# A modulated norm at the head of a two-block transformer kernel: who multiplies the rows of the modulation matrix, and in which order its panels are loaded

## What is computed

```
cond = silu(c)                                    # 1024 values
mod = cond @ w_ada + b_ada                        # w_ada is 1024 x 6144; six parts of 1024
sh1, sc1, gt1, sh2, sc2, gt2 = split(mod, 6)
h = rmsnorm(x, g_mix) * (1 + sc1) + sh1
proj = h @ w_in                                   # its first product: columns C_CQ.., "lat"
```

## Time and profile before

| | |
|---|---|
| median of 3 runs | 796.71 us (796.2 to 798.56) |
| the profiled execution's own time | 800.01 us |
| its span, first to last instruction | 798.0 us |
| PE busy | 95% of the span |
| mean granted clock of PE | 0.981 of full speed |

### The profile page before, as it was taken

One profiled execution on the slowest core, in us unless ns is written; L12 is line 12 of the kernel. 1 busy time (PEld: TensorE's weight loads), 2 busy tenths in 40 slices (PEclk: granted clock), 3 DMA queues, 4 the chain that ended last, 5 costly groups with the idle time before them and its releaser, 6 DMA issues.

```text
span 798.0 us, 14672 instructions
## 1 busy us (share of the span) xinstructions
PE 754.5 (95%) x5310; PEld 691.0 (87%) x5310; DVE 555.9 (70%) x1071; ACT 439.5 (55%) x831; POOL 63.8 (8%) x94
## 2 busy tenths in 40 slices
PE   3699999999999999999999999979899999999997
PEld 3699897899999899999999888867798999999997
DVE  3976449898897866666566755469776877776773
ACT  5327466665645555545545647377665555555452
POOL 8001011000445000000000030000000000000000
PEclk9799999999999999999999999999899999999999
DMA  9977797888796566657657294422153666566531
GB/s 297 346 208 241 188 216 230 266 271 274 253 290 193 146 198 192 194 167 198 195 165 179 58 241 133 139 80 80 54 148 117 211 193 193 166 198 192 167 100 54
DMA packets 186933, 148.24 MB, mean 186 GB/s; under 512 B 13662, under 2 KB 171296, under 8 KB 186872
## 3 DMA queue, kind: packets, MB, share of 16 engines
q1 hardware_dynamic: 183008, 143.61, 61.1%
q10 hardware_dynamic: 2232, 3.03, 2.0%
q0 software_dynamic: 1648, 1.00, 0.5%
HBM read 146.29 MB, written 1.36 MB: 185 GB/s over the span
## 4 chain that ended last, share of the span: by engine, by line
PE 83%; DVE 8%; ACT 5%; issue 2%; DMA 1%; POOL 0%; ACTq 0%; DVEq 0%; POOLq 0%
PE ps L2139 19%; PE ps L1765 15%; PE ps L1766 14%; PE ps L1767 14%; PE ps L2141 10%; DVE w_lo L1135 2%; ACT w_hi L696 1%; DMA arena<-in_x 1%; PE ps L2009 1%; PE ps L2216 1%; PE ps L1831 1%; PE ps L2031 1%; DVE sq L1276 1%; PE ps L1813 1%; PE ps L1996 1%
## 5 line engine op out<-in xcount | busy, mean ns | idle before, releaser
L1135 DVE TENSOR_TENSOR w_lo<-raw,w_hi 128x1024 fp32r<-128x1024 f32 (+3 forms) x223 | 271.1, 1237 | 84.9 <-ACT w_hi L696 83.7
L2139 PE MATMUL ps<-h,w_hi 128*128 128x512 f32 x672 | 239.4, 396 | 0.0
L696 ACT ACTIVATE w_hi<-raw 128x1024 fp32r<-128x1024 f32 (+3 forms) x223 | 226.4, 1038 | 23.3 <-PE ps L1767 13.3
L2141 PE MATMUL ps<-h,w_lo 128*128 128x256 f32 x672 | 189.5, 282 | 0.0
L2139 PEld LDWEIGHTS ps<-h,w_hi 128*128 128x128 f32 x672 | 126.3, 188 | 28.6
L1765 PE MATMUL ps<-h,w_hi 128*128 128x256 f32 (+1 forms) x472 | 137.9, 292 | 5.1 <-ACT bias L1034 1.2
L1766 PE MATMUL ps<-h,w_hi 128*128 128x256 f32 (+1 forms) x472 | 134.1, 284 | 0.0
L1767 PE MATMUL ps<-h,w_lo 128*128 128x256 f32 (+1 forms) x472 | 133.6, 283 | 0.0
L2141 PEld LDWEIGHTS ps<-h,w_lo 128*128 128x128 f32 x672 | 126.2, 188 | 0.0
L1765 PE MATMUL ps<-g_hi,w_hi 128*128 128x256 f32 x352 | 98.7, 280 | 2.6 <-DVE g_lo L1467 2.6
L1765 PEld LDWEIGHTS ps<-h,w_hi 128*128 128x128 f32 (+1 forms) x472 | 90.3, 191 | 10.1 <-issue 7.4
(11 more groups left out here) (353 smaller groups left out, 1120.4 us busy)
## 6 DMA issues: line engine op xcount, KB each, us to landing
raw<-in_w_in SPq DMA_DIRECT2D x53, 512.0 KB, 5.4
raw<-in_w_down SPq DMA_DIRECT2D x44, 512.0 KB, 4.3
raw<-in_w_gate_up SPq DMA_DIRECT2D x44, 512.0 KB, 4.1
raw<-in_w_ada SPq DMA_DIRECT2D x32, 512.0 KB, 4.7
raw<-in_w_gate SPq DMA_DIRECT2D x22, 512.0 KB, 4.0
raw<-in_w_up SPq DMA_DIRECT2D x22, 512.0 KB, 5.1
raw<-in_w_ada SPq DMA_DIRECT2D x32, 256.0 KB, 5.9
raw<-in_w_o SPq DMA_DIRECT2D x8, 512.0 KB, 4.8
```

The costliest lines, as they stand in the source:

```text
L696: A(w_hi[:, m % HL, 0:w], raw[:, n % RAW, 0:w], ACT.Copy).then_inc(hi_done, 1)
L1135: V.tensor_tensor(w_lo[:, m % HL, 0:w], raw[:, n % RAW, 0:w], w_hi[:, m % HL, 0:w].bitcast(f32), sub).then_inc(lo_done, 1)
L2139: T.matmul(bank[:, :], hi, h2[:, k, :, :].rearrange("p a b -> p (a b)"), start=(k == 0), stop=False, skip_group_check=True)
L2141: ins = T.matmul(bank[:, 0:SEQ], lo, h_hi[:, k, :], start=False, stop=(k == KC - 1), skip_group_check=True)
```

## The change

The prologue has three pieces, `PIECES = ((0, 3), (3, 6), (6, 8))`, and a different engine multiplies the rows of each:

- **Piece 0**: eight panels of one row chunk each (768 columns, 393 KB). PE takes rows 0, 2, 4, 6 itself (`first_mod`: the 128x128 blocks of the row as weights, `cond` spread over 128 columns as the moving side), DVE takes rows 1, 3, 5, 7 (`mod_part`); `first_sums` adds DVE's part on PE.
- **Piece 1**: eight such panels, all by DVE, then `second_sums`.
- **Piece 2**: four panels of two rows (512 columns), all by PE (`last_mod`).

The loads come in this order: eight rows of piece 0, `lat0`; three rows of piece 1, `lat1`; three rows, `lat2`; two rows; four panels of piece 2, `lat3`; `lat4` to `lat7`.

PE's order is rows 0 and 2, transposes of `x`, row 4, `rows_t`, `factor`, row 6, `first_sums`, `lat0` to `lat2`, two panels of piece 2, `second_sums`, two panels of piece 2, `lat3`, `lat4`, the bias products, `lat5`, `lat6`, `lat7`. `keep_awake` is not called any more in the prologue.

`c` gets a load and a transpose of its own, ahead of the others; `x` is issued before `b_ada` and `g_mix`; ACT loads its tables for Silu and Sqrt by a dummy call each; the copies of `x` out of PSUM move from ACT to DVE. `scaled` and `low0` become `normal` (x times the inverse norm, made without waiting for the gain) and `h_piece` (sum with gain and shift, then the low part), and ACT makes `h_hi` from the normal and the gain by itself. Elsewhere only semaphores are merged or dropped.

The core of the diff:

```diff
-PIECES = ((0, 2), (2, 4), (4, 6), (6, 7), (7, 8))
+PIECES = ((0, 3), (3, 6), (6, 8))
+MOD_N = (8, 8, 4)
+LAT_PANELS = ((8,), (3, 6), (4,))
...
+        by_pe = q == 2 or (q == 0 and n % 2 == 0)
...
+    done = 0
+    for q in range(len(PIECES)):
+        for n in range(MOD_N[q]):
+            ada_piece(q, n)
+            if n + 1 in LAT_PANELS[q]:
+                lat_panels(done, done + 1)
+                done += 1
+    lat_panels(done, KC)
```

In ACT's program:

```diff
+            split.ahead(0 - AHEAD)
+            for q, (a, b) in enumerate(PIECES):
+                act.wait_ge(s("gain_ready"), q + 1)
+                for c in range(a, b):
+                    line(A(h_hi[:, c, :], sq[:, c, :], ACT.Identity, scale=gs[:, 0, c:c + 1], bias=mod[:, 0, c:c + 1]),
+                         "h_hi")
+                if q < 2:
+                    split.ahead(2 + q - AHEAD)
+            split.ahead(5 - AHEAD)
             act.wait_ge(s("frow_mm"), 2)
...
+            split.ahead(7 - AHEAD)
```

In DVE's program:

```diff
+            for m in mods_of[0][1:4:2]:
+                mod_part(m)
+            for b in range(4):
+                dve.wait_ge(s("x_t"), b + 1)
+                line(V.tensor_copy(xT[:, 2 * b:2 * b + 2, :].rearrange("p a b -> p (a b)"), ps[b][:, :]), "x_copied")
+            inverse(0)
+            for m in mods_of[0][5:8:2]:
+                mod_part(m)
...
+            for c in range(*PIECES[0]):
+                normal(c)
+            split.ahead(0 - AHEAD)
+            dve.wait_ge(s("va_ready"), 1)
+            gain_shift(0)
+            h_piece(0)
+            split.ahead(1 - AHEAD)
+            for m in mods_of[1][0:3]:
+                mod_part(m)
+            split.ahead(2 - AHEAD)
+            for m in mods_of[1][3:8]:
+                mod_part(m)
+            for c in range(*PIECES[1]):
+                normal(c)
+            gain_shift(1)
+            h_piece(1)
+            split.ahead(3 - AHEAD)
+            for c in range(*PIECES[2]):
+                normal(c)
+            gain_shift(2)
+            h_piece(2)
+            split.ahead(7 - AHEAD)
```

In PE's program:

```diff
+            def first_mod(k):
+
+                n = direct_of[k]
+                pe.wait_ge(raw_in[n % RAW], raw_count[n])
+                for x in range(3):
+                    for out_, at_ in ((GAIN0, x * P), (SHIFT0, (3 + x) * P)):
+                        ins = T.matmul(out_[:, x * P:(x + 1) * P], raw[:, n % RAW, at_:at_ + P],
+                                       cond[:, k:k + 1].to_broadcast([P, P]), start=(k == 0 and x == 0), stop=False,
+                                       skip_group_check=True)
+                ins.then_inc(first_used, 1)
+
+            def last_mod(m):
+
+                n, (_, k0, kn, w) = direct_of[m], mod_panels[m]
+                pe.wait_ge(raw_in[n % RAW], raw_count[n])
+                pe.wait_ge(s("gain_ready"), 1)
+                for j in range(kn):
+                    for x in range(4):
+                        ins = T.matmul(ps[4][:, x * P:(x + 1) * P], raw[:, n % RAW, j * w + x * P:j * w + (x + 1) * P],
...
-            for q in range(1, len(PIECES)):
-                mod_sums(q)
-                for k in range(*PIECES[q - 1]):
-                    lat_panel(k)
-                if q <= 2:
-                    keep_awake(ps[6], 2)
```

More of the change, by code:

```diff
@@ L59 @@
 TOKW = GROUP + 2 * HD + FOX_HEADS + 3 * NSA_HEADS
-VA = {"b_ada": 0, "g_mix": 48, "c": 56}
-VA_ROWS = 64
+VA = {"b_ada": 0, "g_mix": 48}
+VA_ROWS = 56
 VB = {"g_ffn": 0, "g_final": 8, "norm_mix_2": 16, "norm_ffn_2": 24, "out_norm_2": 32, "g_q_lora": 40,
@@ L311, in build @@
         x_tm = take(TT, D, start=0)
+        h_sum = arena[:, 0:KC * SEQ].rearrange("p (a b) -> p a b", b=SEQ)
         va_rows = take(P, rows=VA_ROWS)
+        c_rows = take(P, rows=KC)
         vb_rows = take(P, rows=VB_ROWS)
@@ L745, in highs @@
                     high(k, c, shift)
-            split.ahead(AHEAD_OF[1][-1] - AHEAD)
-            act.wait_ge(s("frow_mm"), 2)
[L749 to L757, removed]
+            split.ahead(0 - AHEAD)
[7 more added lines that the diff above has]
+            split.ahead(5 - AHEAD)
+            act.wait_ge(s("frow_mm"), 2)
+            line(A(bias[0:A_HEADS, 0, :], ps[5][0:A_HEADS, 0:FW], ACT.Copy))
+            line(A(bias[0:NSA_HEADS, 1, :], ps[6][0:NSA_HEADS, 0:FW], ACT.Copy), "frow_copied")
+            act.wait_ge(s("rows_t"), 3)
+            line(A(vb[:, :], ps[7][:, 0:VB_ROWS], ACT.Copy), "vb_ready")
+            split.ahead(7 - AHEAD)
             act.wait_ge(s("arg_ready"), 1)
@@ L1178, in mod_part @@
             def mod_part(m):
-                n, (q, k0, kn, w) = direct_of[m], mod_panels[m]
+                n, (q, k, _, w) = direct_of[m], mod_panels[m]
                 dve.wait_ge(raw_in[n % RAW], raw_count[n])
[L1182 to L1192, removed]
+                src, dst = raw[:, n % RAW, 0:w], mod_acc[:, q, :]
@@ new lines, in normal, with h_piece @@
+            def normal(c):
+                line(V.tensor_tensor(sq[:, c, :], xT[:, c, :], NRM, mult))
+            def h_piece(q):
+                a, b = PIECES[q]
+                line.settle()
+                for c in range(a, b):
+                    line(V.tensor_scalar(h_sum[:, c, :], sq[:, c, :], gs[:, 0, c:c + 1], mod[:, 0, c:c + 1], mult, add), "h_ready")
+                for c in range(a, b):
+                    dve.wait_ge(s("h_ready"), c + 1)
+                    dve.wait_ge(s("h_hi"), c + 1)
+                    line(V.tensor_tensor(h_lo[:, c, :], h_sum[:, c, :], h_hi[:, c, :].bitcast(f32), sub), "h_lo")
@@ new lines, in first_sums, with second_sums @@
+            def first_sums():
+                pe.wait_ge(mod_step, mod_used[mods_of[0][-1]][1])
+                for g, out_ in enumerate((GAIN0, SHIFT0)):
+                    for x in range(3):
+                        ins = T.matmul(out_[:, x * P:(x + 1) * P], mod_acc[:, 0, (3 * g + x) * P:(3 * g + x + 1) * P],
+                                       ones[:, 0:P], start=False, stop=True, skip_group_check=True)
+                line(ins, "mod_mm")
+            def second_sums():
+                pe.wait_ge(mod_step, used_by[0])
+                pe.wait_ge(s("gain_ready"), 1)
+                a, b = PIECES[1]
+                for g, out_ in enumerate((GAIN, SHIFT)):
```

192 lines of the change are left out of this document (94 added, 98 removed).

## The result

The changed kernel takes 808.08 us (median of 4 runs, 806.43 to 812.46) where the kernel before takes 796.46 beside it. These two medians are 11.6 us apart; the recorded ratio is 1.0123, interval 1.007 to 1.0176, or 9.8 us (5.6 to 14.0). Run again in another session it gave 808.08 once more, 9.9 us above the kernel before there, and 1.0124 [1.0069, 1.0178]. The prediction was 802.5, range 799.5 to 806: slower, as forecast, but by 10 to 12 us instead of 5.8.

A forecast was written before the change was run, and what follows sets the result against it. PE, busy 95%, bounds the kernel, so its start on `kr` counts: 22.5 to `lat0`, 32.7 of work, 10.6 of pauses give 65.8 against 60.57, +5.3; clock 0.5 makes +5.8. 796.7 + 5.8 = 802.5, range 799.5 to 806.

The forecast's parts named there:

- before `lat1`: PE ahead of `lat1`: its panel lands at 23.4, low part at 25.7, in time for PE (25.3) but for 0.4.
- before the first panel of piece 2: PE after `lat2`: panel 19, issued at 35.0, lands at 39.1 while PE ends at 36.8, a pause of 2.3.
- PE's own work from there to `kr`: PE from `lat0` to `kr`: panels, piece 2, `second_sums` and bias products take 32.7 us together, as before.
- row 2 "can't be there before about 9.4": Head, PE's row 2: estimated from 1.2 MB with `x` taking half the rate; PE free at 12.2.
- The refill of `lat1`: Ring slot 0, freed at 18.8 by PE's row 6: with panels 10 and 11 just ahead, `lat1` lands at 23.4.
- The clock: PE after the long pause before `lat2`: a latent panel costs 5.1 instead of 2.8, mostly absorbed, so 0.5 added.
- The rival of 0.15: PE's clock stays low between the five pauses; two falls cost +3, so 805.5. Chance 0.15.
- step 2: PE before `lat2`: panel 10 holds slot 4, so `lat2` is issued at 27.2, lands at 31.7; a pause of 5.7.
- Ring keeps up: Prologue: early start wins if `lat2` is issued before 21.9 us; `kr` at 55.6, -5, 791.7. Chance 0.08.
- break-even: Prologue: pauses of half the size, 5.4 us in sum, leave the time at 796.7. Chance 0.08.
- The bounds that it lists for its own range: Refill between 3.3 (less 1.7) and 4.8 (plus 2.5), lower clock in head until 19.6 (plus 1.2): +3.5 to +9.
- sign for a mis-sized head: Head: `lat0` starting after 26 would show that the head is mis-sized (rows on PE ahead of `x`), not the ring.

The follow-up runs named there:

- Row 2 to DVE: Changed kernel with row 2 of piece 0 multiplied by DVE, so PE keeps rows 0, 4 and 6; ratio to the kernel before 1.0088 [1.0048, 1.0127].
- latent panels early: Changed kernel with `lat1` and `lat2` loaded right behind `lat0` and split before any row of piece 1; ratio to the kernel before 1.0076 [1.0039, 1.0112].
- after again: The changed kernel run once more without an edit, beside the kernel before; 808.08 us, ratio 1.0124 [1.0069, 1.0178].
- Rows first: Changed kernel with DVE taking five rows of piece 1, not three, before it splits `lat2`; ratio to the kernel before 1.0105 [1.0061, 1.015].
- pause filled: Changed kernel with eleven filler products on PE between `lat1` and `lat2`; ratio to the kernel before 1.0125 [1.0072, 1.0178].
- before, filler: Kernel before with thirteen filler products in PE's six idle us ahead of piece 1's sums; ratio 1.0 [0.9966, 1.0033].
- mended order: Changed kernel, `lat1` and `lat2` right behind `lat0`, bias products moved before piece 2, `lat4` split before piece 2's gain; ratio to the kernel before 1.0027 [0.9995, 1.0059].
- `c` first: Kernel before with half of piece 1's rows and piece 2's last panel on PE, no prologue filler, `c` loaded and transposed first; ratio 0.9938 [0.9904, 0.9972].
- both rows on PE: Kernel before with half of piece 1's rows and piece 2's last panel multiplied by PE, no filler in the prologue; ratio 0.9969 [0.9934, 1.0003].
- rows on PE: Kernel before with the second half of piece 1's rows multiplied by PE in its idle time instead of by DVE; ratio 0.996 [0.993, 0.999].

## Why the direction was right and the size wrong

The mechanism of the pauses was as predicted: PE idle before `lat2` for 5.39 us (predicted 5.7) because slot 4 was held, DVE idle for 4.37 with rows behind the split, DMA rates far below 350 GB/s. All pauses together were 10.0 us where 10.6 were predicted. They were spread otherwise: 1.22 before `lat1` (predicted 0.4, and left out of the sum), none before the first panel of piece 2 (2.3), 1.15 before the second (none). Two things outside the pauses failed: `lat0` started 2.7 us late, and PE's own work from there to `kr` took 35.8 us (45.75 less 10.0) instead of 32.7. Of these 3.1 us half is `lat2` at the lower level; piece 2 with its sums took 9.0 instead of 8.4. By milestones, as differences:

| stretch | predicted | measured | off |
|---|---|---|---|
| start to `lat0` | 22.5 | 25.23 | +2.7 |
| `lat0` to `lat2` | 11.4 | 12.66 | +1.3 |
| `lat2` to piece 2 on PE | 5.2 | 4.39 | -0.8 |
| piece 2 to `lat3` | 9.1 | 10.94 | +1.8 |
| `lat3` to `kr` | 17.6 | 17.76 | +0.2 |

1. **The term that failed is the head's: row 2 "can't be there before about 9.4".** It came at 12.66 (13.1 to 13.7 in the five other executions of this head), so PE, which does nothing else meanwhile, began the transposes at 15.38 and not at 12.2. The estimate counted 1.2 MB of rows and an equal share for `x`. The view of DMA between 0 and 62 us, in 40 slices of 1.55 us, shows how far that rate was right:

```profile
GB/s 0 225 273 339 342 220 348 373 378 320 88 278 398 290 229 300 323 250 30 4 279 213 322 282 0 42 326 204 312 330 353 410 415 373 298 249 157 37 267 293
```

   The first six slices add up to 2.2 MB by 9.3 us, as assumed. Row 2 came only when eight slices had moved 3.3 MB. So some 1.1 MB beside rows 0 to 2 and `x` went first or along with them. Panels issued behind row 2 are a part of it: PE had row 2 at 12.66 and DVE row 3 only 0.9 us later, at 13.56. GpSimd's small loads (0.43 MB up to 62 us) may be another; the shares aren't shown. The Trainium skill ("DMA: Bandwidth & Descriptors", section on issuing engines that are not separate DMA queues) says that DMAs of different issuing engines interleave on the same 16 DMA engines; these rows agree. A row that shows a landing would have been the better source, and one stood there: before, DVE waited until 11.76 for its second panel of 512 KB, and the estimate went below it. Row 2 to DVE supports the price: 2.2 us at `lat0` and 2.6 at `kr`, for the wait and the work together.
2. **The refill of `lat1`**: 5.54 us from issue to landing where 4.6 were taken, with two row panels under way ahead of it and two more issued within 2.2 us behind. `lat2`, with one ahead and two behind, took 4.35 (4.5 taken). The Trainium skill ("DMA: Bandwidth & Descriptors", section on the anatomy of one DMA) gives a fixed 2.0 us and bytes at 436 GB/s, by which it would be 3.2. Both refills on the path were longer, and so was every other load of a latent panel here: 3.9 us at the least in the changed kernel's profile, 3.6 in latent panels early.
3. **The second panel of piece 2**, a wait of 1.15 that no step held: only its first panel was followed. It depends on how long `lat2` runs (after again has none). Rows first shortened the stretch it stands in by 1.1 to 1.3 us.
4. **The clock**: 0.5 us was added, and `lat2` took 4.39 instead of 2.83. Of that nothing is to be had: the time would have been a longer wait for piece 2's panels, as pause filled shows. The rival of 0.15 wanted two falls after step 2, worth 3 us on top; the granted clock shows one, from 37.4 to 40.8, and 1.00 from there to 62. It falls as the cause of what was missing.
5. **Ring keeps up** and **break-even** did not occur: `lat2` was issued at 31.15, where 21.9 would have decided for the first.

The last column here adds up to +5.2, from 65.8 to 70.98. Beside the `kr` of before that is a cost of 10.4 us (11.6 in after again), and the medians say 11.6 and 9.9. In twelve of the thirteen rows below before in the experiments' table the recorded ratio is kinder than `kr` is, by 0.4 to 2.5 us and once by 3.7; in before, filler it is 1.1 the other way. Before's one profile, with `kr` at 60.57, may be an early one: that part is argued.

Two more things in the prediction were wrong in themselves. The bounds that it lists for its own range (less 1.7; plus 2.5 and 1.2) give +4.1 to +9.5 around 5.8, not +3.5 to +9. And its sign for a mis-sized head, `lat0` after 26, did not show (25.23 and 25.89), though the head was 2.7 us late: against its own 22.5, the sign stood at 3.5 us. Its `kr` of 64 to 69 was missed too.

Why does the change lose at all? From `lat0` to `kr` the kernel before needs 29.2 us without a pause worth naming, the changed one 45.75, of which 10.0 are pauses; so the stream itself is 6.6 us longer (rows of piece 2 and bias products stand in it now, and `lat2` at the lower level). `lat0` starts 6.1 us earlier: 10.0 + 6.6 - 6.1 = 10.5. Without pauses the change would thus be worth next to nothing (an estimate: 6.6 - 6.1 = 0.5 us later, with some 1.5 us of the lower level in it): PE has taken on as much as it gained in start. With the mended order (37.4 us from `lat0` to `kr`) and the mended head (`lat0` at 23.1) `kr` would be at 60.5, an estimate from two separate runs, which is where the kernel before stands. The two were not run together.

What pays is PE's idle time used for rows without touching the order of the panels: 0.996 [0.993, 0.999], and 0.9938 [0.9904, 0.9972] with `c` first. That the rows are the cause, and not in part the idle time filled, is argued (see before, filler).

## What to carry to other kernels

Moving work to an idle engine paid here where the order in which buffers come free stayed as it was, and cost where it changed; look first at which slot each later load needs, and who holds it. When a step waits for one of several loads issued together, price it by a row that shows such a landing, and not by its own bytes over the rate. Compare variants by the time between two milestones, since a start that is late by chance (here up to 1.8 us) hides gains of one or two us.

## What the runs showed of the chip

- **The spread of the times goes with the clock's.** From `kr` on all fourteen executions run the same program. Where the records hold 10.3 us at the lower level behind 62 us, that part took 732.6 us (one execution); with some 13.7 us 733.6 to 734.5 (five); with 17.1 us 734.3, 734.4 and 735.6 (three); with 20.6 us 736.3 and 737.4 (two); with some 27.4 us 740.8, 741.0 and 741.0 (three): about half a microsecond for each at the lower level. The places differ from run to run. In the changed kernel PE was busy 48%, 14% and 64% of the few microseconds before the falls at 279.7, 535.7 and 573.2 us, but all of the time before the one at 522.0. The times of one kernel go with it: of both rows on PE the fastest run had 792.55 us at a mean granted clock of 0.991, the slowest 801.91 at 0.979. So a profile with `kr` 1.5 us earlier can show a span 2.1 us longer, as rows on PE does (800.1 against 798.0).
- **The clock before its first event.** In rows on PE the sums of piece 0 take 3.75 us (at 17.50), in both rows on PE 2.02 us (at 16.45), and the clock column reads 1.00 at both places. In that part the pace is the surer reading.
- **Fills of the same size differ**: 4.35 us for the 512 KB of `lat2` with one row panel under way ahead of it, 5.54 for those of `lat1` with two ahead (each with two more issued behind); 9.3 for `x` (1 MB) when six row panels go with it.
